# Retention by chunks: diagonal score blocks and a running 128x128 state per head

## The reference

```python
def retention(q, k, v):           # CHUNK = 64 in the reference
    log_g = jnp.log(1.0 - 2.0 ** (-5.0 - jnp.arange(h)))
    decay_mask = jnp.where(causal, jnp.exp(log_g * (i - j)), 0.0)
    def step(state, inp):
        s = jnp.einsum('bhid,bhjd->bhij', qi, ki) * decay_mask
        intra = jnp.einsum('bhij,bhjv->bhiv', s, vi)
        inter = jnp.einsum('bhid,bhdv->bhiv', qi * q_decay, state)
        new_state = state * chunk_decay + jnp.einsum('bhjd,bhjv->bhdv', ki * k_decay, vi)
        return new_state, intra + inter
...
y_b = head_norm(retention(rq, rk, rv), ret_gn_w, center=True) * jax.nn.silu(rg)
```

## Time and profile before

| | us |
|---|---|
| median of 3 runs | 2685.51 (2685.37 to 2685.70) |
| the profiled execution | 2685.19 |
| its span, first to last instruction | 2683.4 |
| TensorE busy (page) | 2668.1, 99% of the span |
| VectorE busy | 1915.7, 71% |
| ScalarE busy | 1323.4, 49% |
| DMA, mean | 99 GB/s |

### The profile page before, as it was taken

How to read it: one execution, slowest core, us unless ns; L and a number is a source line. 1 busy time by engine, 2 the same in 40 slices (tenths; PEclk the granted TensorE clock), 3 DMA queues, 4 the chain that set the end, 5 groups by cost and what they waited for, 6 DMA issues and landing times.

```text
span 2683.4 us, 41896 instructions
## 1 busy us (share of the span) xinstructions
PE 2668.1 (99%) x17044; PEld 2391.4 (89%) x17044; DVE 1915.7 (71%) x2703; ACT 1323.4 (49%) x1984; POOL 57.0 (2%) x59
## 2 busy tenths in 40 slices
PE   9999999999999999999999999999999999999998
PEld 7887999899988888799989998999988877899987
DVE  6946877688854785687678883588854798688843
ACT  5344644555542534554465562455542467455631
POOL 0020000000000003000000000000000000000000
PEclk9999999999999999999999999999999999999999
DMA  4242332333333324133333333233332430233232
GB/s 150 79 126 65 117 102 79 118 118 100 98 108 89 110 83 130 55 118 106 114 100 107 103 93 104 80 118 99 99 107 90 118 107 2 72 118 111 93 103 80
DMA packets 77216, 266.23 MB, mean 99 GB/s; under 512 B 9600, under 2 KB 12032, under 8 KB 76128
## 3 DMA queue, kind: packets, MB, share of 16 engines
q1 hardware_dynamic: 71136, 254.86, 30.6%
q10 hardware_dynamic: 5888, 8.68, 1.2%
HBM read 251.71 MB, written 4.19 MB: 95 GB/s over the span
## 4 chain that ended last, share of the span: by engine, by line
PE 96%; DVE 2%; ACT 1%; issue 0%; DMA 0%; ACTq 0%; DVEq 0%; SPq 0%
PE bank L504 29%; PE bank L505 29%; PE bank L506 29%; PE bank L2035 1%; PE bank L2013 1%; PE bank L1762 1%; PE bank L1999 1%; PE bank L1778 1%; PE bank L1809 1%; DVE w_lo L690 0%; DVE x L856 0%; DVE u_lo L788 0%; ACT w_hi L686 0%; PE bank L1790 0%; DVE ffn_out L847 0%
## 5 line engine op out<-in xcount | busy, mean ns | idle before, releaser
L504 PE MATMUL bank<-u_hi,w_hi 128*128 128x256 f32 (+1 forms) x2352 | 759.1, 323 | 1.6 <-DVE w_lo L690 0.9
L505 PE MATMUL bank<-u_lo,w_hi 128*128 128x256 f32 (+1 forms) x2352 | 749.5, 319 | 0.0
L506 PE MATMUL bank<-u_hi,w_lo 128*128 128x256 f32 (+1 forms) x2352 | 749.2, 319 | 0.0
L690 DVE TENSOR_TENSOR w_lo<-raw,w_hi 128x1024 fp32r<-128x1024 f32 x250 | 311.7, 1250 | 331.4 <-ACT w_hi L686 330.7
L504 PEld LDWEIGHTS bank<-u_hi,w_hi 128*128 128x128 f32 x2352 | 448.2, 191 | 38.5 <-issue 3.9
L505 PEld LDWEIGHTS bank<-u_lo,w_hi 128*128 128x128 f32 x2352 | 448.2, 191 | 32.6 <-issue 2.4
L506 PEld LDWEIGHTS bank<-u_hi,w_lo 128*128 128x128 f32 x2352 | 448.0, 190 | 31.3
L686 ACT ACTIVATE w_hi<-raw 128x1024 fp32r<-128x1024 f32 x250 | 263.3, 1055 | 332.7 <-PE bank L506 257.4
L505 PE MATMUL bank<-cm,w_hi 128*128 128x256 f32 x1152 | 326.0, 283 | 0.0
L506 PE MATMUL bank<-cm,w_lo 128*128 128x256 f32 x1152 | 326.0, 283 | 0.0
L504 PE MATMUL bank<-cm,w_hi 128*128 128x256 f32 x1152 | 326.0, 283 | 0.0
(11 more groups left out here) (356 smaller groups left out, 4366.2 us busy)
## 6 DMA issues: line engine op xcount, KB each, us to landing
raw<-in_weights SPq DMA_DIRECT2D x314, 512.0 KB, 3.5
rx<-in_weights SPq DMA_DIRECT2D x72, 512.0 KB, 3.5
xr<-in_weights SPq DMA_DIRECT2D x48, 512.0 KB, 3.5
raw<-in_weights SPq DMA_DIRECT2D x32, 384.0 KB, 3.0
rot_s<-rot_in ACTq DMA_DIRECT2D x32, 128.0 KB, 2.4
q_s<-q_in ACTq DMA_DIRECT2D x52, 64.0 KB, 3.1
x<-in_x SPq DMA_DIRECT2D x4, 512.0 KB, 6.5
ret_mask<-in_ret_mask SPq DMA_DIRECT2D x2, 1024.0 KB, 7.4
```

The costliest lines, as they stand in the source:

```text
L504: nc.tensor.matmul(out, st_hi, mv_hi, start=first, stop=False, skip_group_check=onto)
L505: nc.tensor.matmul(out, st_hi, mv_lo, start=False, stop=False, skip_group_check=onto)
L506: return nc.tensor.matmul(out, st_lo, mv_hi, start=False, stop=last, skip_group_check=onto)
L690: nc.vector.tensor_tensor(w_lo[:, bl.slot(p), :], raw[:, bl.raw(p), :], w_hi[:, bl.slot(p), :].bitcast(F32), ALU.subtract).then_inc(lo_spl ...
```

## The change

Scores are now made only inside each 128-token tile (four products of 128 columns). All older tokens reach a tile through a running state: the keys are turned (a transpose on PE, three tiles per head), ACT scales each key by its decay on the way out of PSUM (`ret_keys`, into `ret_kt`), PE multiplies scaled keys by values per tile (`ret_state`, 3 x 128 columns), DVE adds up the tiles (`ret_states`, into `ret_st`), and `ret_out` adds three products of the states with decayed queries to the four within the tiles. DVE makes the decayed queries in `ret_decay`, which otherwise shrinks from four instructions to two.

```diff
     for h in range(HEADS):
-        layer += [(f"s{h}0", 4), (f"s{h}1", 5), (f"s{h}2", 6)]
+        layer += [(f"s{h}0", 4), (f"s{h}1", 5)]
         if h >= 1:
             layer += [(f"out{3 + h}", 7)]
         if h >= 2:
             layer += [(f"var{2 + h}", 6)]
+        layer += [(f"s{h}2", 6)]
...
             def ret_scores(h, li):
                 pe.wait_ge(rot_y.sem, rot_y.upto(li, 4 + h + 1))
+                use = side(f"s{h}1", li)
+                pe.wait_ge(use.drained, use.n + 1)
+                for t in range(TT - 1):
+                    mm = nc.tensor.transpose(use.mem[:, tok(t)], r_k[:, h, tok(t)], ident_c)
+                mm.then_inc(use.filled, 1)
                 use = side(f"s{h}0", li)
                 pe.wait_ge(use.drained, use.n + 1)
...
+                for t in range(TT):
+                    mm = nc.tensor.matmul(use.mem[:, tok(t)], r_k[:, h, tok(t)], r_q[:, h, tok(t)], start=True, stop=True)
+                mm.then_inc(use.filled, 1)
+
+            def ret_state(h, li):
+                keys = side(f"s{h}1", li)
+                pe.wait_ge(keys.drained, keys.n + 2)
+                if h == 0:
+                    pe.wait_ge(rv_cent.sem, rv_cent.upto(li, 4))
                 use = side(f"s{h}2", li)
                 pe.wait_ge(use.drained, use.n + 1)
...
+                for t in range(TT - 1):
+                    mm = nc.tensor.matmul(use.mem[:, tok(t)], ret_kt[:, t, :], r_v[:, t, tok(h)], start=True, stop=True)
+                mm.then_inc(use.filled, 1)
 
             def ret_out(h, li):
-                for i in range(3):
+                for i in (0, 2):
...
+                for t in range(TT):
+                    nc.tensor.matmul(use.mem[:, tok(t)], r_v[:, t, tok(h)], within[:, tok(t)], start=t == 0, stop=False)
+                for t in range(TT - 1):
+                    mm = nc.tensor.matmul(use.mem[:, tok(t + 1)], ret_st[:, t, :], later[:, tok(t)], start=False, stop=t == TT - 2)
...
                 for h in range(HEADS):
                     project(GR + h)
+                    if h == 1:
+                        ret_state(0, li)
                     ret_scores(h, li)
                     if h >= 1:
                         ret_out(h - 1, li)
                     if h >= 2:
                         head_var(2 + h, li)
+                    if h >= 1:
+                        ret_state(h, li)
...
+            def ret_keys(h, li):
+
+                use = side(f"s{h}1", li)
+                act.wait_ge(use.filled, use.n + 1)
+                for t in range(TT - 1):
+                    decay = par[:, P_KDEC + 3 * h + t:P_KDEC + 3 * h + t + 1]
+                    keys = nc.scalar.activation(ret_kt[:, t, :], use.mem[:, tok(t)], ACT.Copy, scale=decay)
+                keys.then_inc(use.drained, 1)
...
                 for h in range(HEADS):
                     split(GR + h)
+                    ret_keys(h, li)
                     gate_silu(h, ou, li)
...
+            def ret_states(h, li):
+
                 use = side(f"s{h}2", li)
                 dve.wait_ge(use.filled, use.n + 1)
+                nc.vector.tensor_copy(ret_st[:, 0, :], use.mem[:, tok(0)]).then_inc(ret_sum.sem, 1)
+                dve.wait_ge(ret_sum.sem, ret_sum.upto(li, 2 * h + 1))
+                nc.vector.tensor_tensor(ret_st[:, 1, :], use.mem[:, tok(1)], ret_st[:, 0, :], ALU.add).then_inc(ret_sum.sem, 1)
+                dve.wait_ge(ret_sum.sem, ret_sum.upto(li, 2 * h + 2))
+                nc.vector.tensor_tensor(ret_st[:, 2, :], use.mem[:, tok(2)], ret_st[:, 1, :], ALU.add).then_inc(use.drained, 1)
...
                     split(GR + h)
+                    if h >= 2:
+                        ret_states(h - 1, li)
                     gate_in(h, bl, ou, li)
+                    if h == 1:
+                        ret_states(0, li)
                     ret_decay(h, li)
...
+                ret_states(3, li)
                 square_low(6, li)
```

More of the change, by code:

```diff
@@ L47 @@
 HALF = P // 2
+RET_LATER = T - P
+RET_AT = 2 * P - 1
 Q_IN = 6
@@ L104 @@
 G_NEXT, G_MIX_POST, G_FFN_PRE, G_FFN_POST = 0, 8, 16, 24
-P_CONV, P_RETGN, P_GLAGN, P_BA, P_WGA = 32, 44, 48, 52, 54
+P_CONV, P_RETGN, P_GLAGN, P_BA, P_KDEC, P_WGA = 32, 44, 48, 52, 54, 66
 N_PAR = P_WGA + KD * RANK
@@ L300, in build @@
         ret_mask = region("ret_mask", [P, HEADS, T], 36)
-        s_ret = region("s_ret", [P, 2, 1280], 16)
+        s_ret = region("s_ret", [P, 2, T + RET_LATER], 16)
+        ret_kt = region("ret_kt", [P, TT - 1, P], 23)
+        ret_st = region("ret_st", [P, TT - 1, P], 25)
         yc_hi = region("yc_hi", [P, 4, T], 16, F32R)
@@ L418, in build @@
         rv_cent = ev("rv_cent", 4)
+        ret_sum = ev("ret_sum", 2 * HEADS)
         hn_sq = ev("hn_sq", 8)
@@ L1799, in ret_out @@
             def ret_out(h, li):
-                for i in range(3):
+                for i in (0, 2):
                     src = side(f"s{h}{i}", li)
                     pe.wait_ge(src.drained, src.n + 2)
-                if h == 0:
-                    pe.wait_ge(rv_cent.sem, rv_cent.upto(li, 4))
                 use = side(f"out{4 + h}", li)
                 pe.wait_ge(use.drained, use.n + 1)
-                s = s_ret[:, h % 2, :]
-                for kt, a, b in ((0, 0, 512), (1, 512, 896), (2, 896, 1152), (3, 1152, 1280)):
-                    mm = nc.tensor.matmul(use.mem[:, tok(kt, TT - kt)], r_v[:, kt, tok(h)], s[:, a:b], start=kt == 0, stop=kt == 3)
+                within, later = s_ret[:, h % 2, 0:T], s_ret[:, h % 2, T:]
@@ L2245, in gate_high @@
                     nc.scalar.activation(w_hi[:, bg.slot(p), :], gate_weights(bg, li, t, i), ACT.Copy).then_inc(hi_split, 1)
-                src = side(f"s{HEADS - 1}2", li)
-                act.wait_ge(src.filled, src.n + 1)
+                src = side(f"s{HEADS - 1}0", li)
+                act.wait_ge(src.drained, src.n + 2)
                 mixed_high(G_T4)
@@ L2581, in ret_decay @@
                 dve.wait_ge(use.filled, use.n + 1)
[L2582 to L2586, removed]
+                nc.vector.tensor_tensor(s[:, T:], r_q[:, h, P:], mask[:, P:], ALU.mult)
+                tiles = [ap.rearrange("p (a n) -> p a n", a=TT) for ap in (s[:, 0:T], use.mem[:, :])]
+                within = mask[:, 0:P].rearrange("p (o n) -> p o n", o=1).to_broadcast([P, TT, P])
+                nc.vector.tensor_tensor(tiles[0], tiles[1], within, ALU.mult).then_inc(use.drained, 1)
+            def ret_states(h, li):
                 use = side(f"s{h}2", li)
                 dve.wait_ge(use.filled, use.n + 1)
-                nc.vector.tensor_tensor(s[:, 896:1152], use.mem[:, 0:256], mask[:, 0:256], ALU.mult).then_inc(use.drained, 1)
+                nc.vector.tensor_copy(ret_st[:, 0, :], use.mem[:, tok(0)]).then_inc(ret_sum.sem, 1)
[3 more added lines that the diff above has]
+                nc.vector.tensor_tensor(ret_st[:, 2, :], use.mem[:, tok(2)], ret_st[:, 1, :], ALU.add).then_inc(use.drained, 1)
             def layer(li):
@@ L3130, in per_partition @@
     return v.reshape(-1, P).T
+RET_LOG = np.log(1.0 - 2.0 ** (-5.0 - np.arange(HEADS)))
 def layer_parameters(a):
@@ L3139, in layer_parameters @@
         cols += [per_partition(a[n][li]) for n in ("ret_gn_w", "gla_gn_w", "gla_b_a")]
+        cols += [np.exp(lg * (RET_AT - np.arange(RET_LATER))).astype(np.float32).reshape(TT - 1, P).T for lg in RET_LOG]
         cols += [a["w_in"][li][:, 5120:5120 + RANK].reshape(KD, P, RANK).transpose(1, 0, 2).reshape(P, KD * RANK)]
@@ L3161, in constants @@
         masks.append(mask[:, np.arange(P) % lev >= lev // 2].astype(f))
-    c = np.arange(T)[None, :] - np.arange(P)[:, None]
-    log_g = np.log(1.0 - 2.0 ** (-5.0 - np.arange(HEADS)))
-    decay = [np.where(c >= 0, np.exp(lg * np.maximum(c, 0)), 0.0).astype(f) for lg in log_g]
+    c = i - j
+    later = np.broadcast_to(np.arange(P, T) - RET_AT, (P, RET_LATER))
+    decay = [np.concatenate([np.where(c >= 0, np.exp(lg * np.maximum(c, 0)), 0.0), np.exp(lg * later)], axis=1).astype(f) for lg in RET_LOG]
     inv = np.power(f(10000.0), -np.arange(HD, dtype=f) / f(HD)).astype(f)
```

2 lines of the change are left out of this document (removed).

## The result

| | us |
|---|---|
| before, median of 6 runs | 2685.48 (2685.37 to 2685.70) |
| changed, median of 6 runs | 2710.86 (2708.87 to 2711.65) |
| ratio, with its 95% interval | 1.0094 (1.0083 to 1.0104) |
| span of the profiled execution, before and changed | 2683.4 and 2709.5 |

The change costs 25.4 us. The direction was forecast; the size was not: +8.5 was forecast, and 2710.86 lies outside 2691 to 2701. What follows shows that the 25.4 are three things: the forecast's own sum (about 9), TensorE's falling clock, which the forecast had left to rival 1 (about 9), and about 8 us from a term that it had put at nothing.

The account below looks back on a forecast made before the run. The prediction took PE's stream of products plus a few short gaps to bound the kernel. From the profiled 2685.19 us, - 7.0 (stream) + 15.4 (bank 6 waits) + 0.1 gave 2693.7, against the median 2694.0; range 2691 to 2701.

Parts of the forecast that it names:

- the forecast's own sum: Whole kernel: 7.0 us gained by the stream, 15.4 lost to waits and 0.1 in step 1, giving 2694.0 us.
- rival 1: At the bank 6 waits the clock falls too, 2.5 us each time: 2696.5 with one fall, 2704 with four; chance 0.20.
- The stream: PE's products in the retention loop: 3.45 us per head instead of 4.33, so 7.0 us gained over eight heads.
- The wait on bank 6: Steps 2 and 3: the state product waits until ACT reads the sum of squares, 3.75 and 3.95 us, 15.4 over two layers.
- T: The end of the projection in a step of the retention loop, from which the forecast counts its times.
- The keys: Step 3: ACT's three key copies ahead of the silu table load, taken as 0.65 us, holding 0.2 us of the wait.
- The 12 more columns of parameters are nothing.: Parameter tiles: the 12 added columns were claimed to cost no time.
- The price of a wait: Bank 6 waits in steps 2 and 3: the likeliest case counted 15.4 us lost, with no clock fall included.
- They are short beside the 5.4 us of dense work on both sides: Argument against the clock falling in the four gaps of 3.7 to 3.9 us, which stand between projections of 5.4 us.
- The wait in step 1: Before the output, PE waits for DVE's sum of head 0's state: 0.05 us per layer, bounds 0 and 0.3.
- Narrow products that cost 0.62 of wide ones: Estimate from the skill page for 128-column products: 7.4 us per head, some 27 us more lost; the forecast rejected it.
- rival 3: Weight loads of the narrow products set the pace at full length, 5.7 us a head: 18 us more, 2712; chance 0.02.

Follow-up runs that it names:

- The shift alone: The kernel before with one unused tile of 160 bytes per partition behind the parameters, nothing else changed: 2693.42 us, ratio 1.0029.
- the fill kernel: Changed kernel with 96 unused bytes, plus 15 useless 512-column products between sum of squares and state in steps 2 and 3: 2694.81 us.
- the first two kernels with bank 5: Changed kernel with the states of heads 1 to 3 in bank 5, 2689.27 us; the same with 96 unused bytes behind the parameters, 2681.14 us.

## Why the prediction was wrong

- **The stream, -7.0 forecast.** Right: 2678.46 against 2685.46.
- **The wait on bank 6, +15.4 forecast.** Right in place, number and size: four waits, 14.7 us of idle time and the restarts, 15.4 by the two steps of layer one taken twice. PE arrived at T + 3.25 and moved at T + 6.96 in step 2 (forecast 3.23 and 6.98); in step 3, T = 256.77, it moved at 263.98, T + 7.21 (forecast 7.16). The keys took 0.90 there rather than 0.65, from 257.29 to the table load at 258.19, but ACT's copy of the output came only 0.11 late (260.03, T + 3.26), and the way from there to PE's start was 3.95 rather than 4.00.
- **"The 12 more columns of parameters are nothing."** This step failed: +8.0. I counted the columns' bytes and not what they push. The shift alone reproduces it (2693.42).
- **The price of a wait.** This step failed too, and by as much: the sum prices a wait by its idle time alone and puts the clock behind it at nothing, leaving it to rival 1 with a chance of 0.20. The clock fell in all four gaps. That is about 9 us, 2.3 each where rival 1 had 2.5: the two loops lost 17.9, of which the fill kernel lost 8.9 without a fall. An estimate from the granted clock agrees: 3.4 and 6.8 us less 0.9 idle, at half rate and in two layers, are 9.3. "They are short beside the 5.4 us of dense work on both sides" was no argument, since all four fell in spite of it, and 2.2 and 2.4 us of idle time were enough once each. The kernel before had a sign that the prediction didn't read: after PE's last product (its end is 2674.7) the clock still stands at 1.00 from 2675 to 2679, and at 0.54 from 2679 to 2683. Rival 1's 2704 is what was measured where the addresses play no part (2702.25); with them it would have been 2712. The Trainium skill (TensorE: Matmul & The Clock Gate, "HAM oscillation — how this bites in real kernels"), which I cited and gave too little weight, says that idle gaps between bursts bring half rate each time; here the trace agrees for the gaps of 3.5 to 3.8 us, four falls in four; for those of 2.2 and 2.4 us it was two in four.
- **The rest.** The wait in step 1, put at 0.05 us per layer, is no longer than 0.1: L1824 takes 0.96 us until L1826 starts there (234.18 to 235.14) against 0.90 in step 2 (243.19 to 244.09). Narrow products that cost 0.62 of wide ones, by which the stream would have been 27 us longer than before, were not seen: eight records of 128 columns again take 0.89 us (242.30 to 243.19). The same row speaks against rival 3; that its 2712 lies next to the measured 2710.86 is chance.

Put together: 8.9 (stream and waits: what the fill kernel lost in its two retention loops) + 9 (clock) + 8.0 (addresses) = 25.9 between the traces, 25.4 in the medians. Either of the last two alone would have carried the forecast's 2694.0 past 2701. The three were separated by experiments; the clock's 9 in the changed kernel itself is a difference of two traces, and between the medians with and without the filling it is 7.4.

## What to carry to other kernels

Follow a bank or buffer to its next user when the order of uses changes: here a state placed behind a sum in one bank made TensorE wait for the slowest chain of the step, and moving it to a bank that is waited for anyway took the wait and the half clock away (2710.86 to 2689.27). With the large area at a shift of 256 bytes and the sum of states put earlier the loss became a gain of 7. Price a wait of TensorE with the half clock behind it, not by its idle time alone. And when a kernel whose time is all matrix products gains or loses what nobody can place, compare the same untouched instruction group in both profiles: a parameter tile that grows moves every tile behind it, and 64 or 160 bytes were worth -6 and +8 us here.

## What the runs showed of the hardware that I had not expected

- Rounded-fp32 products of 512 columns on the hidden tiles took 226 to 236 ns, and those of 256 columns on `cm` 117.4 to 120.0, by where the tiles that TensorE reads lie relative to one another; at a shift of 64 or 160 bytes the narrow ones gain where the wide ones lose.
- The clock fell at gaps of 3.5 to 3.8 us each time, at gaps of 2.17 and 2.42 us in one of two layers each, and never at the 1.3 us that every trace has once or at the 1.1 to 1.2 us in front of the transposes in the first two kernels with bank 5. At half clock 512-column products start every 0.43 us, and each stretch lasted 3.4 or 6.8 us, of which PE was idle for 1.1 us at most.
- Stretches of 3.4 and 6.8 us at half clock leave no mark in the page's 40 slices; the mean granted clock of the run, 0.995 against 0.999, does show them.
